# A gating projection by Strassen's products in a one-core decoder trunk: weight sums by transfers, a residual row by transfers, token sums later

## What is computed

```python
def chunked_spatial_gating(x, w_in, b_in, ln_g, ln_b, w_s, b_s, w_out, b_out):
    bsz, t, _ = x.shape
    z = jax.nn.gelu(x @ w_in + b_in, approximate=False)
    u, v = jnp.split(z, 2, axis=-1)
    v = layer_norm(v, ln_g, ln_b)
    ...
    s = jnp.einsum("gts,bnsgc->bntgc", w_causal, v) + b_s.T[:, :, None]
    s = s.reshape(bsz, t, GMLP_HALF)
    return (u * s) @ w_out + b_out

def reference(x, ...):
    for i in range(DEPTH):
        ...
        x = layer_norm(DEEPNORM_ALPHA * x + y, norm1_g[i], norm1_b[i])
        y = conv_ffn(x, ffn_w_up[i], ffn_b_up[i], ffn_w_dw[i], ffn_b_dw[i],
                     ffn_w_down[i], ffn_b_down[i])
        x = layer_norm(DEEPNORM_ALPHA * x + y, norm2_g[i], norm2_b[i])
    return x
```

## Time and profile before

| | us |
|---|---|
| median of three runs | 1015.83 (1014.35 to 1017.22) |
| the profiled execution | 1015.58 |
| its span, first to last instruction | 1013.8 |
| TensorE busy in the span | 1003.6 |
| VectorE busy | 867.6 |
| ScalarE busy | 604.5 |
| GpSimd busy | 233.3 |

### The profile page before, as it was taken

How to read it: one execution, slowest core, us unless ns; L and a number is a source line. 1 busy time by engine, 2 the same in 40 slices (tenths; PEclk the granted TensorE clock), 3 DMA queues, 4 the chain that set the end, 5 groups by cost and what they waited for, 6 DMA issues and landing times.

```text
span 1013.8 us, 15746 instructions
## 1 busy us (share of the span) xinstructions
PE 1003.6 (99%) x5379; PEld 861.1 (85%) x5379; DVE 867.6 (86%) x1228; ACT 604.5 (60%) x903; POOL 233.3 (23%) x289
## 2 busy tenths in 40 slices
PE   9999999999999999999999999999999999999997
PEld 7777788988899988888888888898988999888885
DVE  6999977897988988898894878779888888879888
ACT  7889865564565556666454343457555555566653
POOL 2998730023232121000010210002423212100001
PEclk9999999999999999999999999999999999999999
DMA  9766269369889676376555333825989966627652
GB/s 342 218 161 166 58 147 349 119 196 238 236 211 228 220 169 173 102 271 208 195 179 194 118 111 107 307 79 186 262 237 229 220 209 173 163 98 260 205 197 112
DMA packets 65590, 194.02 MB, mean 191 GB/s; under 512 B 7552, under 2 KB 8576, under 8 KB 65024
## 3 DMA queue, kind: packets, MB, share of 16 engines
q1 hardware_dynamic: 44144, 137.76, 39.1%
q0 software_dynamic: 19376, 48.24, 23.7%
q10 hardware_dynamic: 2016, 7.34, 2.1%
HBM read 178.11 MB, written 54.53 MB: 229 GB/s over the span
## 4 chain that ended last, share of the span: by engine, by line
PE 78%; DVE 5%; DMA 3%; issue 2%; ACT 1%; SPq 0%; DVEq 0%; POOL 0%; POOLq 0%; ACTq 0%
PE ps L2017 10%; PE ps L2018 10%; PE ps L2019 10%; PE ps L2306 6%; PE ps L2307 6%; PE ps L2308 6%; PE ps L2259 5%; PE ps L2260 5%; PE ps L2261 5%; PE ps L2027 4%; PE ps L2028 4%; PE ps L2029 4%; DMA raw<-d_weights 3%; PE ps L2186 1%; DVE ps L1618 1%
## 5 line engine op out<-in xcount | busy, mean ns | idle before, releaser
L2017 PE MATMUL ps<-xh,wh 128*128 128x512 f32 x528 | 208.5, 395 | 0.3 <-DVE wl L1280 0.3
L2018 PE MATMUL ps<-xl,wh 128*128 128x512 f32 x528 | 205.7, 390 | 0.0
L2019 PE MATMUL ps<-xh,wl 128*128 128x512 f32 x528 | 205.6, 389 | 0.0
L767 ACT ACTIVATE wh<-raw 128x1024 fp32r<-128x1024 f32 x114 | 119.9, 1057 | 80.4 <-PE ps L2308 49.5
L1280 DVE TENSOR_TENSOR wl<-raw,wh 128x1024 fp32r<-128x1024 f32 x101 | 123.2, 1224 | 32.9 <-ACT wh L767 32.5
L702 POOL DMA_DIRECT2D summed<-d_weights x88 | 75.2, 1115 | 198.0 <-PE ps L2019 96.4
L2017 PEld LDWEIGHTS ps<-xh,wh 128*128 128x128 f32 x528 | 99.2, 188 | 22.0 <-issue 1.2
L2019 PEld LDWEIGHTS ps<-xh,wl 128*128 128x128 f32 x528 | 99.1, 188 | 21.0
L2018 PEld LDWEIGHTS ps<-xl,wh 128*128 128x128 f32 x528 | 99.2, 188 | 20.7 <-issue 1.2
L2306 PE MATMUL ps<-wh,parts 128*128 128x512 f32 x264 | 102.9, 390 | 0.0
L2308 PE MATMUL ps<-wh,parts 128*128 128x512 f32 x264 | 102.7, 389 | 0.0
(11 more groups left out here) (266 smaller groups left out, 2543.9 us busy)
## 6 DMA issues: line engine op xcount, KB each, us to landing
raw<-d_weights SPq DMA_DIRECT2D x156, 512.0 KB, 4.9
raw<-summed SPq DMA_DIRECT2D x56, 512.0 KB, 4.1
summed<-d_weights POOLq DMA_DIRECT2D x88, 256.0 KB, 9.5
summed<-d_weights SPq DMA_DIRECT2D x66, 256.0 KB, 5.2
summed<-summed POOLq DMA_DIRECT2D x46, 256.0 KB, 4.8
res<-brow POOLq DMA_DIRECT2D x12, 512.0 KB, 10.7
wl<-raw POOLq DMA_DIRECT2D x4, 1024.0 KB, 6.9
wl<-raw POOLq DMA_DIRECT2D x5, 512.0 KB, 6.3
```

Of the source, the lines that this page charges most:

```text
L767: eng.activation(split_at(u)[0], raw[:, u % RAW, :], ACT.Copy).then_inc(w_hi, 1)
L2017: eng.matmul(ps[:, bank, cols], a, xh[:, k, cols], start=(k == 0), stop=False)
L2018: eng.matmul(ps[:, bank, cols], a, xl[:, k, cols], start=False, stop=False)
L2019: mm = eng.matmul(ps[:, bank, cols], b, xh[:, k, cols], start=False, stop=(k == KD - 1))
```

## The change

- v's 8 units become 14: four with blocks B11 and B21 side by side (`gv_units`), two made of W21 - W11 and so on for the product of A22, four for the fifth and sixth product, four for the third and seventh, all sums from `gsum`. u's first unit moves between them (`U_GU0`).
- The sums are made in DRAM: SP issues three copies behind each of the loads of `U_CONV_OUT` + 0 to 3 (12 of 256 KB), GpSimd issues the adds and copies between the roots of the first normalization and `up_sums(0)`, in five rounds which wait for each other and a last one that nothing there waits for.
- The token sums are made by VectorE (`gn5`, `gs2`) and GpSimd (`gs4`, `gv7`), their high parts by ScalarE, their low parts by VectorE. ScalarE keeps four blocks and two halves of blocks (`block_kept`, `second_kept`).
- VectorE combines the seven products in `vtm` with 20 operations of 128 x 512. GpSimd adds the two halves of the bias row (`both_rows`) after the last round of the down-projection.
- The residual's row: ScalarE scales `brow` by 1/ALPHA, GpSimd adds it to `res` by four accumulating transfers, `half_sum` multiplies by ALPHA. `residual(2)` goes.
- Small loads (`gvrow`, `glg`, `wsraw`) move to other places of ScalarE's queue.

```diff
@@ SP
+        def gv_copies(i):
+            w1, w2 = weights_d[raw_gv + i], weights_d[raw_gv + GQ + i]
+            eng.dma_start(gsum_d[2 + i, :, 0:HALF], w1[:, 0:HALF]).then_inc(gv_copied, 16)
+            eng.dma_start(gsum_d[2 + GQ + i, :, HALF:UNIT], w2[:, 0:HALF]).then_inc(gv_copied, 16)
+            eng.dma_start(gsum_d[2 + GQ + i, :, 0:HALF], w2[:, HALF:UNIT]).then_inc(gv_copied, 16)
...
+            if u == U_GV + GQ:
+                eng.wait_ge(gv_sum, 16 * (4 + 2 * GQ))
             load(u % RAW, u)
+            if 0 <= u - U_CONV_OUT < GQ:
+                gv_copies(u - U_CONV_OUT)
@@ GpSimd
         for t in range(NT):
             norm_root(ROOTS + t, t + 1, t)
+        eng.wait_ge(gv_copied, 16 * 3 * GQ)
+        eng.dma_start(fifth[:, :, first], w2[:, :, first], accum_op=ALU.add).then_inc(gv_sum, 16)
+        eng.dma_start(third[:, :, second], w2[:, :, second], accum_op=ALU.add).then_inc(gv_sum, 16)
+        eng.wait_ge(gv_sum, 16 * 2)
+        eng.dma_start(fifth[:, :, second], fifth[:, :, first]).then_inc(gv_sum, 16)
+        eng.wait_ge(gv_sum, 16 * 3)
+        eng.dma_start(fifth[:, :, second], w2[:, :, second], accum_op=ALU.add).then_inc(gv_sum, 16)
+        eng.wait_ge(gv_sum, 16 * 4)
+        for i in range(GQ):
+            eng.dma_start(gsum_d[i // 2, :, second if i % 2 else first], fifth[i, :, second]).then_inc(gv_sum, 16)
+        eng.wait_ge(gv_sum, 16 * (4 + GQ))
+        for i in range(GQ):
+            eng.dma_start(gsum_d[i // 2, :, second if i % 2 else first], w1[i, :, second], accum_op=ALU.add).then_inc(gv_sum, 16)
         up_sums(0)
+        eng.wait_ge(gv_in, 16)
+        eng.wait_ge(w_used, U_GV - FOURTH)
+        eng.tensor_tensor(both_rows[:, :], gvrow[:, 0:HALF], gvrow[:, HALF:D], ALU.add).then_inc(rows_ok, 1)
         for t in range(NT):
             norm_root(ROOTS + NT + t, NT + t + 1, t)
+        eng.wait_ge(br3_ok, 1)
...
+        for t in range(NT):
+            eng.dma_start(res[:, t, :], brow[:, :], accum_op=ALU.add).then_inc(res3_add, 16)
+        eng.wait_ge(w_used, U_GV + GQ)
+        eng.wait_ge(x_kept, 2 * NT)
+        eng.wait_ge(*lo_of(U_G56 + 1))
+        for t in range(NT // 2):
+            cols = slice(t * P, (t + 1) * P)
...
+            eng.tensor_tensor(gs4[:, :, cols], gs2[:, :, cols], a12f[:, :, cols], ALU.add).then_inc(ga_more, 1)
+            eng.tensor_tensor(gv7[:, :, cols], gs2[:, :, cols], a22f[:, :, cols], ALU.add).then_inc(ga_more, 1)
@@ ScalarE
+        eng.activation(brow[:, :], brow[:, :], ACT.Copy, scale=1.0 / ALPHA).then_inc(br3_ok, 1)
+        token_hi(gn5h, gn5, 0, ga_sum, 1)
+        token_hi(gs2h, gs2, 0, ga_sum, 2)
+        his([U_G56])
+        token_hi(gn5h, gn5, 1, ga_sum, 3)
+        token_hi(gs2h, gs2, 1, ga_sum, 4)
+        his([U_G56 + 1])
+        gelu_v(0, 0, G_C11 - 1)
+        gelu_v(1, 0, G_C11)
+        row(glb[:, :], R_GLB, gm_in)
+        his([U_G56 + 2])
+        gelu_u(0)
+        his([U_G56 + 3])
+        for t in range(NT // 2):
+            token_hi(gs4h, gs4, t, ga_more, 2 * t + 1)
+            token_hi(gv7h, gv7, t, ga_more, 2 * t + 2)
+        his([U_G37, U_G37 + 1])
@@ VectorE
+        los([U_GU0])
+        eng.wait_ge(x_kept, 2 * NT)
+        for t in halves:
...
+            eng.tensor_tensor(gn5[:, :, cols], ps[:, B0[1] + 2 * t, :].rearrange("p (k n) -> p k n", k=4), a22f[:, :, cols],
+                              ALU.subtract).then_inc(ga_sum, 1)
...
+            eng.tensor_tensor(gs2[:, :, cols], gn5[:, :, cols], a11f[:, :, cols], ALU.subtract).then_inc(ga_sum, 1)
+        eng.wait_ge(ga_sum, 4)
+        token_lo(gn5l, gn5, gn5h, 0, 1)
+        token_lo(gs2l, gs2, gs2h, 0, 2)
+        los([U_G56])
+        los([U_G56 + 1])
+        token_lo(gn5l, gn5, gn5h, 1, 3)
+        token_lo(gs2l, gs2, gs2h, 1, 4)
+        los([U_G56 + 2])
+        eng.wait_ge(w_used, U_GU0)
+        eng.wait_ge(rows_ok, 1)
+        for t in halves:
+            eng.tensor_tensor(vtm[:, 2 + t, c2], vtm[:, 2 + t, c1], both_rows[:, :], ALU.subtract).then_inc(n_ok, 1)
+        eng.wait_ge(n_ok, NT // 2)
+        for t in halves:
+            eng.tensor_tensor(vtm[:, 2 + t, c1], ps[:, 4 + t, :], vtm[:, 2 + t, c1], ALU.add).then_inc(gv_rd, 1)
+        los([U_G56 + 3])
@@ TensorE
+        def gv(u, c, bank, tokens, i, t):
+            h, l = split_at(u)
+            w_h, w_l = h[:, c * HALF:(c + 1) * HALF], l[:, c * HALF:(c + 1) * HALF]
+            s_h, s_l = [x[:, i, t * P:(t + 1) * P] for x in tokens]
+            eng.matmul(ps[:, bank + t, :], s_h, w_h, start=(i == 0), stop=False)
+            eng.matmul(ps[:, bank + t, :], s_h, w_l, start=False, stop=False)
+            return eng.matmul(ps[:, bank + t, :], s_l, w_h, start=False, stop=(i == GQ - 1))
...
+        for pair in range(GQ // 2):
+            for t in range(NT // 2):
+                eng.wait_ge(ga_lo, 2 * t + 2)
+                for i in (2 * pair, 2 * pair + 1):
+                    u = U_G56 + i
+                    if t == 0:
+                        eng.wait_ge(*lo_of(u))
+                    gv(u, 0, 0, gn5p, i, t)
+                    mm = gv(u, 1, 2, gs2p, i, t)
```

294 lines of the change are left out of this document (219 added, 75 removed).

## The result

| | before | after |
|---|---|---|
| median, us | 1015.53 (1014.35 to 1017.22, 4 runs) | 1025.89 (1025.46 to 1026.84, 4 runs) |
| the profiled execution, its span | 1015.58, 1013.8 | 1025.46, 1023.7 |
| TensorE busy | 1003.6 (5379 matmuls) | 1001.1 (5355) |
| VectorE, ScalarE, GpSimd busy | 867.6, 604.5, 233.3 | 888.0, 618.4, 256.1 |

The account below looks back on a forecast made before the run. TensorE's instruction stream was taken as the bound, busy 1003.6 of 1013.8 us. Terms -5.4 + 0.8 + 2.7 + 0.9 + 2.4 = +1.4 gave a 1017.2 us median, called same; range 1011 to 1021.

Parts of the forecast that it names:

- Matmuls saved: Gating projection of v: 168 matmuls instead of 192, taking 5.4 us from TensorE's stream; called certain.
- The weight sums' transfers: Layer 0's up-projection loop: gating sums delay layer 0's sums to about 226, slowing the load at 264; 2.4 us of waiting.
- No later load pays: Up-projection loop: loads after the one at 264 cost nothing, since copies follow, at 5.4 us a load.
- The earlier ones, from 218.4 on: Up-projection loop: the load at 218.4 meets copies or adds either way; taken as 0, bounds -1 and +4.
- Rival (b): Up-projection loop decides: loads at 12.5 us; first step 4.7 us gives 1019.5, a further 4.8 gives 1024.3; chance 0.23.
- Its other ground: Weight sums: the big transfers might use few DMA engines and take four times as long; part of the 0.23 chance.
- GpSimd beside VectorE: Gating, fifth and sixth products: four GpSimd additions lengthen VectorE operations by 0.91 each, 3.6 us, of which 2.7 reach TensorE.
- the 0.7 of the feed: Gating: the low part of the fifth and sixth products' fourth unit ends 0.7 us after TensorE wants it.
- my walk: Gating: VectorE and ScalarE instruction prices laid in program order from 537.11; TensorE waits 0.8 us without other hindrance.
- both_rows: End of the down-projection, about 508.2: GpSimd's bias-row sum meets VectorE's full chain once; 0.9 us, bounds 0 and 1.3.
- What was taken as free: Plain copies, residual transfers, row scaling and additional unit loads, at several places, counted as no cost; some bounded 0 to 2.
- SyncE's copies at 85 to 97: Twelve plain copies behind the output projection's loads: taken as free, bounds 0 and 2 us.

Follow-up runs that it names:

- e18: e9 without copies or transfers for the gating weight sums, raw weights loaded in their place, so the output is not the reference's; 1016.0 us, ratio 0.9998.
- e15: The kernel before with one more GpSimd wait holding back layer 0's own weight sums, no gating sums; 1018.19 us, ratio 1.0018.
- e6: The changed kernel with the four token-sum additions (gs4, gv7) on VectorE instead of GpSimd; 1025.16 us, ratio 1.0106.
- e4: The changed kernel with VectorE's low part of the fifth and sixth products' fourth unit ahead of the row subtractions and evictions; 1028.75 us, ratio 1.0126.
- e5: The changed kernel with e4's move, gating sums behind layer 0's sums, residual transfers behind token sums, both_rows behind the second normalization's roots; 1022.25 us, ratio 1.0076.
- e7: The changed kernel with e5's three GpSimd moves, token-sum additions on VectorE, and VectorE's and TensorE's gating order changed; 1018.47 us, again 1018.66 us.
- e9: e7 with both_rows added by VectorE and the low part of the gating's fourth early unit one step earlier; 1017.31 us, ratio 1.0015.
- e14: e9 with SyncE's copies moved to the down-projection and the gating sums as 24 serial transfers of 256 KB; 1044.72 us.

## Why the prediction was wrong

**Matmuls saved: right.** 24 fewer. e18, with most of what stood against them away, gains 2.6 us in the gating; 2.8 still go there to waits of 0.42, 0.65 and 0.68 us and to smaller ones.

**The weight sums' transfers: the place was right, the size wrong (2.4 forecast, 5.6 measured).** The first step that failed is the length of the rounds. I priced them from adds of 256 KB alone on the engines, 12.9, about 5, 7.7 and about 6 us, with some 8 for other transfers and issuing; measured were 20.4, 8.8, 13.8 and 8.1 us, so the sums of layer 0 started at 240 and not at 226. The second is "No later load pays" and the load that I followed, at 264 alone. The earlier ones, from 218.4 on, which I held to be indifferent (-1 to +4), took 10.9 us for 8.8 and began a row of three slow turns, and the loads at 309 to 316 took 12.1 for 8.5: TensorE waited at 246, 266, 289 and 333, not at 284. And late sums of layer 0, on which my 2.4 rested, cost 0.4 us by themselves (e15, 23 us late where I had 8). Rival (b) named the loop and 1019.5 to 1024.3 us; of the loop's part, 4.7 by its first step and 9.5 by its second, the 5.6 are close to the first, but its load at 290 was quick (4.3 us). Its other ground did not appear: the transfers of 1 MB weren't four times as long, 20.4 us for the first two together (2 MB) against 12.9 worked out, and from 190 to 206 us, when only these two were on GpSimd's queue, its packets kept 83% of the 16 engines busy, which is 13 and not twice 4. The rule of the Trainium skill that I put beside it (DMA: Bandwidth & Descriptors, why a DMA increments its semaphore by 16), by which the slowest dimension limits the number of engines, can't be held against that, since how the transfer was cut up is not in the trace.

**GpSimd beside VectorE: right in mechanism, 2.7 forecast; e6 shows the longer rows.** Meetings lengthened single operations by 1.1 us each (1.79 for 0.68, 2.31 for 1.22, two of 3.48 for 1.28), 4.4 in all instead of 3.6, with no idle time of VectorE to take it in. With the 0.7 of the feed I had 3.4 us for the wait ahead of the fourth unit; it was 3.15. That these are so near is partly luck: 4.4 and 0.7 are 5.1, so the rest of my walk was some 2 us too dear for VectorE. e4 and e6 show that a third term was just behind it, the loads, so what VectorE lost isn't what TensorE would get back: with the additions on VectorE the stage took 1.6 us more.

**both_rows: right, 0.9 forecast.** One part row of VectorE read 1.52 us, and 0.66 and 0.29 us of waits at 524 to 527 are gone when it stands behind the roots (e5, e7).

**What was taken as free and wasn't.** (1) The first unit products of the gating: TensorE now takes only the left half of each unit for the first block of tokens, so it wants the fourth unit 2.0 us after the first instead of 4.1; its low part came 0.96 late (e9). My walk put this unit nowhere, since these four units were "as before"; but their use was not. (2) The transfers of the residual, the rows and the units together: loads of 11.1 us, a cost hidden only by the VectorE wait. (3) SyncE's copies at 85 to 97: a wait of 0.26 us at 101.54 in the changed kernel, and 0.4 to 1.6 us at 100 us in five of the versions, within my 0 to 2. (4) The end, 2.1 us, in no term at all.

**The sum.** -5.4 + 3.3 (gating, with what is under 0.3 us) + 1.1 (start of the gating) + 1.1 (both_rows) + 5.5 (loop) + 2.1 (end) = 7.7 us, of which forecast: -5.4 + 0.8 + 2.7 + 0.9 + 2.4 = 1.4. The misses are 3.1 in the loop, 2.1 at the end and 1.1 at the stage's start. The other 2.2 us of the profiled difference are the slow start, which the kernel before shows too in other executions, and the medians differ by 2.7 more than this sum, which no run places. With the 7.7 alone the time would be 1023.3 us, beyond the range too. My range held the bounds of each cost, but hardly their sum: all but one were on the dear side.

## What to carry to other kernels

Price a burst of transfers from a stretch as full as the one it will stand in, not from one transfer alone, and put it where the DMA engines have room: here the same sums cost TensorE 5.6 us ahead of the loop, 0 to 3.8 behind it in bursts, and 0.5 to 0.7 in two chains. Ask also what stands behind it on its queue: here four transfers of 512 KB came late and met the next burst. A consumer that takes its operands in another order than before sets new due times for units that the change leaves as they are; walk those too. And an addition that is moved to an idle GpSimd isn't free where VectorE is full: four of 0.7 us cost 4.4 us of VectorE. But taking them back was worth nothing to TensorE until its order and VectorE's were changed too (e6, e7), since the loads were the next bound.

## What the runs showed of the hardware that I had not expected

A wait of TensorE of 2 to 3 us could bring the granted clock to 0.50 right behind it, at 1.7 us each, in some executions and not in others; behind e14's wait of 29 us it was at 0.52 from 546 to 552. Nearly the same instruction stream reached the first mark between 168.6 and 172.9 us in twenty profiles, by how fast single loads landed. And GpSimd's closing drain has at least two lengths, 3.75 and 6.5 to 6.7 us, and where it is long it decides when the program ends.
